# The first loads in another order: x in four pieces, units 0 and 2, the first weight job, then units 1 and 3

## The reference

```
silu_c = jax.nn.silu(c)
silu_cc = jax.nn.silu(c_ctx)
sh1, sc1, g1, sh2, sc2, g2 = split(silu_c @ mod_w[layer] + mod_b[layer])       # six vectors of 1024
csh1, csc1, cg1, csh2, csc2, cg2 = split(silu_cc @ mod_w[layer] + mod_b[layer])
h = rmsnorm(x, norm_mix_g[layer]) * (1.0 + sc1) + sh1
x = x + g1 * fourier_conv_mixer(h, ...)
...
def fourier_conv_mixer(h, w_in, conv_w, conv_b, conv_g, w_out):
    pa, pu, pg = jnp.split(h @ w_in, [512, 1024], axis=-1)
    ya = real part of the FFT of pa over tokens and over each group of 128 features
    u = pu * jax.nn.sigmoid(pg)
    u = a convolution of u over 31 tokens, by feature, + conv_b
    yb = jax.nn.silu(rmsnorm(u, conv_g))
    return jnp.concatenate([ya, yb], axis=-1) @ w_out
```

## Time and profile before

| | |
|---|---|
| time, median of 3 runs | 3025.89 us (3021.37 to 3025.99) |
| the profiled execution's own time | 3025.73 us |
| its span | 3023.8 us |
| PE busy | 2843.4 us (94%) |
| VectorE busy | 1054.0 us (35%) |
| ScalarE busy | 754.7 us (25%) |
| chain that ended last, by engine | PE 77%, DMA 10%, VectorE 6%, ScalarE 3% |

### The profile page before, as it was taken

How to read it: one execution, slowest core, us unless ns; L and a number is a source line. 1 busy time by engine, 2 the same in 40 slices (tenths; PEclk the granted TensorE clock), 3 DMA queues, 4 the chain that set the end, 5 groups by cost and what they waited for, 6 DMA issues and landing times.

```text
span 3023.8 us, 37135 instructions
## 1 busy us (share of the span) xinstructions
PE 2843.4 (94%) x15882; PEld 1964.4 (65%) x15882; DVE 1054.0 (35%) x2096; ACT 754.7 (25%) x1311; POOL 487.9 (16%) x499
## 2 busy tenths in 40 slices
PE   7989899999979999979999988999999889999997
PEld 4778756544548765765454536888865556888876
DVE  5973300000053343320000015343276554432334
ACT  4142211111142154311111114222111264321223
POOL 0000122332200044023333310000043140000000
PEclk9989999999989999989999999999999999999998
DMA  8513999999942132369999983222211201322321
GB/s 294 195 46 109 378 377 418 426 427 426 419 155 82 56 126 88 138 264 412 426 427 425 426 346 138 99 98 98 103 58 44 102 1 56 111 98 92 103 84 49
DMA packets 142794, 621.54 MB, mean 206 GB/s; under 512 B 15981, under 2 KB 97005, under 8 KB 108960
## 3 DMA queue, kind: packets, MB, share of 16 engines
q0 software_dynamic: 42592, 403.76, 32.0%
q1 hardware_dynamic: 98880, 210.35, 19.9%
q10 hardware_dynamic: 1152, 4.98, 0.4%
HBM read 624.26 MB, written 27.79 MB: 216 GB/s over the span
## 4 chain that ended last, share of the span: by engine, by line
PE 77%; DMA 10%; DVE 6%; ACT 3%; issue 1%; POOL 1%; SPq 1%; DVEq 0%; POOLq 0%; ACTq 0%
PE ps L92 75%; DMA ring<-in_exp_up,wix 6%; PE ps L95 2%; DMA ring<-in_exp_down,wix 2%; DVE scr L114 2%; ACT hT L98 1%; SPq L132 1%; DVE xT L114 1%; DVE scr L106 1%; DVE hT L110 1%; ACT ring_r L102 0%; DVE scr L117 0%; POOL scr L110 0%; POOL ring L110 0%; DVE ring_r L106 0%
## 5 line engine op out<-in xcount | busy, mean ns | idle before, releaser
L92 PE MATMUL ps<-ring_r 128*128 128x512 f32 (+1 forms) x2688 | 769.3, 372 | 6.1 <-DVE hT_r L106 4.1
L92 PEld LDWEIGHTS ps<-ring_r 128*128 128x128 f32 x2688 | 490.6, 189 | 112.7 <-issue 18.5
L92 PE MATMUL ps<-hT_r,ring_r 128*128 128x512 f32 (+1 forms) x1256 | 468.4, 373 | 0.0
L92 PE MATMUL ps<-ring,scr 128*64 128x512 f32 (+4 forms) x2112 | 452.1, 537 | 16.9 <-DMA ring<-in_exp_up,wix 13.3
L92 PE MATMUL ps<-scr_r,ring_r 128*128 128x512 f32 x1312 | 306.7, 390 | 0.3 <-issue 0.3
L92 PEld LDWEIGHTS ps<-ring,scr 128*64 128x64 f32 (+2 forms) x2112 | 164.4, 142 | 216.9 <-issue 203.8
L106 DVE TENSOR_TENSOR scr<-scr,ps 64x512 f32<-64x512 f32 (+1 forms) x76 | 52.5, 691 | 674.2 <-ACT scr L98 448.2
L92 PEld LDWEIGHTS ps<-scr_r,ring_r 128*128 128x128 f32 x1312 | 246.3, 188 | 52.3 <-issue 0.5
L92 PEld LDWEIGHTS ps<-hT_r,ring_r 128*128 128x128 f32 x1256 | 237.2, 189 | 41.2 <-issue 0.7
L106 DVE TENSOR_TENSOR ring_r<-ring,ring_r 128x2048 fp32r<-128x2048 f32 (+1 forms) x102 | 225.2, 2230 | 90.1 <-ACT ring_r L102 89.6
L92 PE MATMUL ps<-ring,hT 128*64 128x512 f32 (+3 forms) x928 | 229.3, 526 | 12.4 <-DMA ring<-in_exp_up,wix 8.3
(11 more groups left out here) (165 smaller groups left out, 2920.7 us busy)
## 6 DMA issues: line engine op xcount, KB each, us to landing
ring<-in_ffn_w SPq DMA_DIRECT2D x66, 1024.0 KB, 5.3
ring<-in_mod_w SPq DMA_DIRECT2D x12, 2048.0 KB, 7.9
ring<-in_mod_w SPq DMA_DIRECT2D x24, 1024.0 KB, 5.3
ring<-in_exp_up SPq DMA_DIRECT2D x4, 2048.0 KB, 10.6
ring<-in_exp_down SPq DMA_DIRECT2D x4, 2048.0 KB, 8.6
ring<-in_exp_gate SPq DMA_DIRECT2D x4, 2048.0 KB, 12.2
ring<-in_w_in SPq DMA_DIRECT2D x4, 2048.0 KB, 8.3
ring<-in_w_cd SPq DMA_DIRECT2D x6, 1024.0 KB, 6.0
```

What stands on the lines that cost most here:

```text
L92: return self.real.matmul(o, l, r, start=start, stop=stop) if self.real else Quiet()
```

## The change

SyncE now loads vec, kon, x in four pieces of two tiles each (each with a semaphore of its own), unit 0, unit 2, the first job, unit 1 and unit 3, then as before. ScalarE issues no load and squares a tile when its piece is there. On PE the head is the norm and then units 0 and 2 with their turns. Units 1 and 3 and their turns stand in block 0, behind tiles 1, 2 and 3; the three half units stand together behind tile 7; four products of constants are left in place of eight. VectorE and ScalarE make the first four tiles from units 0 and 2 and the last four from units 1 and 3 (`half_gains(0)`, `half_gains(1)`), each in an order written out by hand. The arithmetic is the same.

```diff
-    vec_in, const_in, x_in, out_done = (signal(x) for x in ("vec_in", "const_in", "x_in", "out_done"))
+    vec_in, const_in, out_done = (signal(x) for x in ("vec_in", "const_in", "out_done"))
+    x_in = [signal(f"x_pair{q}_in") for q in range(4)]
...
-    mod0 = Mod("first", 0, [0, 1, 2, 3], s_)
+    mod0 = Mod("first", 0, [0, 2, 1, 3], s_)
...
-        for j in range(3):
+        for j in (1, 2):
             job(j)
-        e.wait_ge(*ps.filled("mod", 0, 2))
+        e.wait_ge(*ps.filled("mod", 0, 1))
...
-                if kt in (2, 5):
-                    mods(0, kt // 3)
-            mods(0, 2)
-            mods(0, 3)
+                if kt == 1:
+                    pe_mod_unit(e, mod0, 1)
+                if kt == 2:
+                    pe_mod_turn(e, mod0, 1)
+                    pe_mod_unit(e, mod0, 3)
+                if kt == 3:
+                    pe_mod_turn(e, mod0, 3)
+            for g in range(4):
+                mods(0, g)
             wr.done(("f", 0), "f_up", 0, 512)
-        pe_turn_over(e, "f", 8)
+        pe_turn_over(e, "f", 4)
...
+        def shift(kt):
+            for r, (a, n) in enumerate(chunks(768)):
+                e.wait_ge(*h_scaled.of("f_in", kt, a))
+                i = e.activation(H(kt, a, n), H(kt, a, n), ACT.Identity, bias=mod(0, 0, kt, r))
+            i.then_inc(*h_ready.up("f_in", kt))
+
+        def upper(kt):
+            e.wait_ge(*h_ready.of("f_in", kt))
+            e.copy(f_in(kt)[0], H(kt)).then_inc(*h_hi.up("f_in", kt))
+        for kt in (0, 4):
+            shift(kt)
+            upper(kt)
+            shift(kt + 1)
+            shift(kt + 2)
+            upper(kt + 1)
+            shift(kt + 3)
+            upper(kt + 2)
+            upper(kt + 3)
         part_upper(e, ("f", 1))
-        act_adaln(e, "f_in", 0, 0, 768, st_x0, f_in, normed=True)
...
+        def half_gains(half):
+            e.wait_ge(*ps.emptied("mod_t", 0, half))
+            e.wait_ge(*ps.emptied("mod_t", 0, 2 + half))
+            o = MT[:, 0:32].rearrange("p (w h j r) -> p w h j r", w=2, h=2, r=2)[:, :, half]
+            b = vec("mod_b", 0, 16).rearrange("p (w h j) -> p w h j", w=2, h=2)[:, :, half, :, None].broadcast_to([128, 2, 4, 2])
+            e.tt(o, o, b, ADD).then_inc(*dve_step.up("mod_b", "first", half))
+            e.wait_ge(*dve_step.of("mod_b", "first", half))
+            sc = MT[:, 16 + 8 * half:24 + 8 * half].rearrange("p (k r) -> p k r", r=2)
+            g = vec("nmix", 4 * half, 4)[:, :, None].broadcast_to([128, 4, 2])
+            e.stt(AM[:, 8 * half:8 * half + 8].rearrange("p (k r) -> p k r", r=2), sc, 1.0, g, ADD, MUL).then_inc(
+                *dve_step.up("f_in", "am", half))
+            e.wait_ge(*dve_step.of("f_in", "am", half))
+
+        def scale(kt):
+            for r, (a, n) in enumerate(chunks(768)):
+                e.wait_ge(*root_there(st_x0, a))
+                e.stt(H(kt, a, n), X(kt, a, n), AM[:, 2 * kt + r:2 * kt + r + 1], root(st_x0, a, n), MUL, MUL).then_inc(
+                    *h_scaled.up("f_in", kt, a))
+
+        def lower(kt):
+            hi, lo = f_in(kt)
+            e.wait_ge(*h_hi.of("f_in", kt))
+            e.tt(lo, H(kt), hi.bitcast(F32), SUB).then_inc(*h_lo.up("f_in", kt))
+        mod_row(e, mod0, 0)
+        mod_columns(e, mod0, 0)
+        mod_row(e, mod0, 2)
+        mod_columns(e, mod0, 2)
+        half_gains(0)
+        scale(0)
+        scale(1)
         part_lower(e, ("f", 0))
-        dve_adaln(e, "f_in", 0, 0, "nmix", 768, st_x0, f_in, normed=True)
...
-        for u, s in zip(mod0.units, (0, 1, 2, 5)):
+        for q in range(4):
+            e.dma(xT[:, 1536 * q:1536 * q + 1536].rearrange("p (k t) -> p k t", k=2), I["xT"][:, 2 * q:2 * q + 2, :]).then_inc(
+                *x_in[q].up("x", by=16))
+        def mod_unit(u, s):
             weights_load(e, s, ("mod", 0, u), I["mod_w"][0, u], 8, 512)
+        mod_unit(0, 0)
+        mod_unit(2, 1)
+        raw_load(e, 3, ("f", 0), *F.jobs[0])
+        mod_unit(1, 2)
+        mod_unit(3, 5)
...
-        pe_mod_unit(e, mod0, 0)
         pe_norm_sum(e, st_x0)
-        pe_mod_unit(e, mod0, 1)
         pe_norm_root(e, st_x0)
-        for u in (2, 3):
-            pe_mod_turn(e, mod0, u - 2)
+        for u in (0, 2):
             pe_mod_unit(e, mod0, u)
-        for u in (2, 3):
             pe_mod_turn(e, mod0, u)
...
-        e.dma(xT[:, :].rearrange("p (k t) -> p k t", k=8), I["xT"]).then_inc(*x_in.up("x", by=16))
         e.wait_ge(*vec_in.of("vec"))
         act_mod_begin(e, mod0)
-        e.wait_ge(*x_in.of("x"))
         for o in st_x0.order:
+            e.wait_ge(*x_in[o[0] // 2].of("x"))
             act_square(e, st_x0, *o)
...
-            if o == (5, 512, 256):
-                mod_row(e, mod0, 0)
         dve_norm(e, st_x0)
-        mod_row(e, mod0, 1)
-        for u in (2, 3):
-            mod_columns(e, mod0, u - 2)
-            mod_row(e, mod0, u)
-        for u in (2, 3):
-            mod_columns(e, mod0, u)
-        dve_mod_bias(e, mod0)
-        e.wait_ge(*dve_step.of("mod_b", "first"))
-        e.wait_ge(*x_in.of("x"))
+        for q in range(4):
+            e.wait_ge(*x_in[q].of("x"))
```

More of the change, by code:

```diff
@@ L900, in dve_fourier @@
     def dve_fourier(e):
-        part_lower(e, ("f", 0))
-        dve_adaln(e, "f_in", 0, 0, "nmix", 768, st_x0, f_in, normed=True)
+        def half_gains(half):
[26 more added lines that the diff above has]
+        scale(1)
+        part_lower(e, ("f", 0))
+        lower(0)
+        scale(2)
+        lower(1)
+        scale(3)
+        lower(2)
+        mod_row(e, mod0, 1)
+        lower(3)
+        mod_columns(e, mod0, 1)
+        mod_row(e, mod0, 3)
+        mod_columns(e, mod0, 3)
+        half_gains(1)
+        scale(4)
+        scale(5)
+        lower(4)
+        scale(6)
+        lower(5)
+        scale(7)
+        lower(6)
+        lower(7)
         part_lower(e, ("f", 1))
```

## The result

The changed kernel takes 3041.01 us (median of 4 runs, 3037.61 to 3044.51) where the one before takes 3024.28 (median of 4, 3021.37 to 3025.99): a ratio of 1.0054, 95% interval 1.0043 to 1.0066, so 13 to 20 us slower. The profiled execution took 3039.64 us, 13.9 more than that of before; its span is 3037.6.

What follows compares the result with a forecast made beforehand. Transfers were taken to bound up to 41.6 us, then PE alone from 49.23 to 132.55. Head -5.05, block 0 +18.0 and clock +2 gave +15 on 3025.73: 3040.7 us, range 3029 to 3048.

Steps and rivals of the forecast that it cites:

- +15 us at the take-over: Where VectorE takes over the chain with the convolution (132.55 before): -5.05 + 18.0 + 2 = +15 us.
- The transfers: Loads at the start: x's quarters land near 8.3, 10.2, 12.1 and 14.0 us, unit 0 stays at 19.0.
- The head: Up to the first product: half clock taken from 17.4 us, first scaling 36.2, first product 41.7 against 46.75, 5.05 gained.
- the rival at the full clock throughout: Stalls smaller, no measurable change: first product at 35.5 (-6.2), reload hidden, +2.5, 3028 us; chance 0.10.
- Block 0: PE from first product to start of m = 1: 38.9 us instead of 20.9, so +18.0 before the clock's cost.
- The term for the alternation: VectorE and ScalarE in block 0: one turn takes 3.45 us a tile where PE needs 2.2, idle 1.25.
- The +2 for the clock: Half clock on PE behind block 0's idle stretches: +2 us, from 0 (full) to 5 (half behind each long gap).
- The reload: Third half unit's load, issued once PE has used the first: lands 5.2 us later with hops, PE idle 4.25.
- The convolution: VectorE's convolution starts near 76.9 instead of 67.2, +9.7; PE stays on the chain, VectorE waits about 6 us.
- the transfers are the whole bound: Rival: faster, engines' chains fit inside PE's work; first product at 34.0 gives -7 us, 3018.8; chance 0.05.
- No change: Rival: stalls smaller, no measurable change, with the reload hidden by another transfer order; +2.5, 3028 us; chance 0.10.
- One for one: What PE's work up to 132 us loses or gains passes to the kernel's end in full.

Runs made afterwards that it cites:

- run 4: Changed kernel with ten products of constants instead of three in the warm-up at the start: 3037.29 us.
- run 3: Changed kernel with VectorE scaling three tiles before the first lower part in the second four tiles, then one ahead: 3037.51 us.
- run 6: Changed kernel with four unread products of constants before tile 4 and four before the third half unit, block 0's banks held: 3035.87 us.
- run 7: Changed kernel's loads, PE and VectorE reordered against all stalls: 3027.46 us; with ten warm-up products too, 3020.82, ratio 0.9985 to the kernel before.
- run 5: Kernel before with only x's loads changed, four pieces on SyncE's queue in front of the units: 3020.94 us.
- run 1: Changed kernel with the first two half units behind tiles 4 and 5, block 0's banks held: 3037.08 us; retimed 3036.12, ratio 1.0036.

## Why the prediction was right

The forecast was 3040.7; 3041.01 was measured, and +15 us at the take-over came out as +14.94.

- **The transfers.** A landing of x's first quarter near 8.3 and of unit 0 near 19 were 8.3 and 18.9. The last quarter, issued at 3.2, took 10.7 us and landed at 13.9, where the forecast had 14.0. The rule of the Trainium skill (DMA: Bandwidth & Descriptors, Bandwidth), 1 MiB per DMA for 75% of the peak, put the last near 16.7, an estimate from that figure; the trace does not bear it out for pieces of 0.75 MiB that stand behind each other in one queue.
- **The head.** The choice of the half clock for 17 to 29 us was the one that mattered: sums 5.28 and root 2.93 were there, unit 0 took 3.19 against 3.5 chosen. First scaling 36.09 (36.2), first product 41.51 (41.7). By run 4 the full clock for the sums alone would have given 38.21. The 35.5 of the rival at the full clock throughout was a slip in the sum: by the forecast's own terms the full clock saves 2.4 in the sums, 1.3 in the root and 1.6 in unit 0, so 5.3 and not 6.2, which gives 36.4.
- **Block 0.** 40.4 us to the start of m = 1, where 38.9 and 2 for the clock were forecast. The wait before tile 4 was 4.55 (4.25), that for the third half unit 4.43 (4.25). The term for the alternation was right in its cause (run 3) but counted idle time that partly was not there: the half clock made tiles 0 and 4 so slow that PE waited 0.35 us instead of 1.25 before tile 1. Clock and idle time were forecast as if they added up; they overlapped. The +2 for the clock is near what run 6 gives, 1.8 behind the two long gaps.
- **What the terms were worth.** From the first product to the take-over: 85.80 us before, 105.98 with the change, 98.93 with the half units spread, 91.77 and 91.79 in the versions of run 7. The remaining 6 us over before fit units 1 and 3 with their turns, which are 5.7 us by their rows in the changed kernel (forecast 5.95); no run takes them out of the block alone. The reload and its neighbours cost 7.05, the place of the units and the order on VectorE the other 7.2, in which the half clock behind the wait before tile 4 is counted.
- **The convolution** started at 77.21 (76.9), behind ScalarE's copy of unit 4's row, and was not the bound: VectorE then waited 4.84, 1.20 and 0.42 us for PE (forecast about 6).
- **The rivals.** That the transfers are the whole bound, and an earlier start of them decides, fell with run 5 for x alone, whose order on VectorE had also stayed; with the stalls taken out and the longer warm-up (run 7) the sign does turn, by 4.4 us where that rival had 7. No change would have needed a hidden reload, which run 1 shows only with another order.
- **One for one.** The shift at the take-over passed through: +14.37 at the issue of the router's weights (293.05 before, 307.42 now), +13.8 at the end of the profiled pair, 16.7 between the medians. Between, the two executions wandered (+10.0 at the second such issue, 1272.64 against 1282.68). As the stretch behind the take-over varies by over 10 us among the eleven executions, the agreement of the end with the forecast to 0.3 us is luck; the 15 us at 150 us are not.

## What to carry to other kernels

An earlier start is worth only what stays in front of it: list every step that moves from ahead of the first product to behind it, and give each a place where the engine would idle anyway. Where two or three loads take turns in one buffer, their users must stand apart by at least the time of a load; put together behind a block, they turn a hidden transfer into a wait. And write orders by hand for the slower pair of engines: in the second four tiles one scaling less ahead made VectorE's turns 3.55 us, where with it they are 2.4 and 1.7 (run 3).

## What the runs showed of the hardware

- x alone on its own queue held up what was beside it: the small vectors took 10.2 us to land there and 2.7 in front of x in one queue, the constants 13.0 and 4.9.
- The same head ran with a unit 0 of 1.94, 2.17, 2.39, 2.15, 2.77, 2.96 and 3.19 us in seven executions of kernels that do not differ up to there: when the granted clock comes back varies from one execution to the next, and moved the first product by up to 1.3 us. In the same order the warm-up had ended at 10.90, 11.03, 11.29, 11.46, 12.05, 12.07 and 12.10 us, so a late end went with a late return of the clock; no run tests whether it is the cause.
- A dense stretch of products up to the start of the short ones did not hold the clock through them: in run 4 it was granted in full until 21 us and then fell, as the products of the root began.
